# A hybrid decoder step on one core: the samples' recurrence moved to an earlier stage, gates by tanh, another order of loads and final stores

## What is computed

```python
u = _rmsnorm(tok, norm_mix[l]) @ w_in[l]
bg, cg, hv, q, fx, iv, og = jnp.split(u, SPLIT_POINTS, axis=-1)
y_conv = cg * conv            # conv: width 3 over bg * hv
f = lb + (1 - lb) * sigmoid(fx);  kk = 1 - f
S_new = exp(b_last) * S0 + k~^T v;  o = scores @ v + (q * exp(b)) @ S0
y_rec = rmsnorm_per_head(o) * rec_gain * silu(og)
h = h + concat(y_conv, y_rec) @ w_out
for e in range(32): out += combine[:, e] * (act(x @ w1[e] + b1[e]) @ w2[e] + b2[e])
y_prompt, y_sample = rmsnorm(h), also the new convolution rows and the new states
```

## Time and profile before

| | us |
|---|---|
| runs of the kernel before | 1114.75, 1112.18, 1114.08 |
| their median | 1114.08 |
| the profiled execution's own time | 1113.06 |
| its span, first to last instruction | 1111.3 |
| busy PE, weight loads, DVE, ACT, POOL | 1051.9, 465.3, 268.1, 171.5, 24.7 |
| bytes moved by DMA | 431.94 MB |
| granted clock of TensorE, mean | 0.994 of full |

### The profile page before, as it was taken

One profiled execution on the slowest core, in us unless ns is written; L12 is line 12 of the kernel. 1 busy time (PEld: TensorE's weight loads), 2 busy tenths in 40 slices (PEclk: granted clock), 3 DMA queues, 4 the chain that ended last, 5 costly groups with the idle time before them and its releaser, 6 DMA issues.

```text
span 1111.3 us, 12051 instructions
## 1 busy us (share of the span) xinstructions
PE 1051.9 (95%) x5212; PEld 465.3 (42%) x5212; DVE 268.1 (24%) x527; ACT 171.5 (15%) x412; POOL 24.7 (2%) x63
## 2 busy tenths in 40 slices
PE   7999999999999999999999989899998999999996
PEld 6767855343434334343433324243434343433332
DVE  5657634221111212020201012121212020202122
ACT  3562004120201011110110102020101010101102
POOL 3000012000000000000000000000000000000000
PEclk9999999999999999999999999999999999999998
DMA  9942379999999999999999999999999999999994
GB/s 304 354 177 76 143 277 392 408 428 427 428 428 426 429 426 428 428 427 428 428 427 428 425 431 426 427 428 427 429 428 427 429 426 428 425 431 426 429 420 170
DMA packets 50873, 431.94 MB, mean 389 GB/s; under 512 B 5238, under 2 KB 16190, under 8 KB 25120
## 3 DMA queue, kind: packets, MB, share of 16 engines
q1 hardware_dynamic: 48800, 428.54, 92.6%
q0 software_dynamic: 608, 2.04, 0.6%
q10 hardware_dynamic: 1408, 0.54, 0.2%
HBM read 427.63 MB, written 3.48 MB: 388 GB/s over the span
## 4 chain that ended last, share of the span: by engine, by line
PE 60%; DMA 36%; DVE 2%; issue 1%; ACT 0%; SPq 0%; DVEq 0%
DMA ring<-in_expert_w 35%; PE ps L1884 28%; PE ps L1939 8%; PE ps L1501 6%; PE ps L1806 3%; PE ps L1479 3%; PE ps L1780 2%; PE ps L1627 2%; PE ps L1569 1%; PE ps L1790 1%; PE ps L1859 1%; DMA ring<-in_x_prompt 1%; PE ps L1721 1%; PE ps L1808 0%; PE ps L1713 0%
## 5 line engine op out<-in xcount | busy, mean ns | idle before, releaser
L1884 PE MATMUL ps<-ring,mem 128*64 128x512 f32 x2048 | 461.7, 600 | 19.7 <-DMA ring<-in_expert_w 19.7
L1884 PEld LDWEIGHTS ps<-ring,mem 128*64 128x64 f32 x2048 | 146.1, 137 | 303.2 <-issue 302.1
L1939 PE MATMUL ps<-ring,mem 128*64 128x512 f32 x1024 | 223.7, 594 | 4.0 <-ACT mem L850 3.7
L1302 DVE TENSOR_TENSOR mem<-mem,ps 128x1024 f32<-128x1024 f32 x30 | 36.6, 1221 | 449.6 <-PE ps L1806 415.4
L1939 PEld LDWEIGHTS ps<-ring,mem 128*64 128x64 f32 x1024 | 72.3, 137 | 143.6 <-issue 136.1
L1501 PE MATMUL ps<-ring 128*128 128x266 f32 (+1 forms) x320 | 77.0, 397 | 2.0 <-DVE ring L970 1.5
L855 ACT ACTIVATE mem<-ps 128x264 f32<-128x264 f32 x16 | 6.3, 391 | 448.5 <-PE ps L1859 448.5
L1780 PEld LDWEIGHTS ps<-mem 128*128 128x128 f32 x600 | 65.4, 173 | 13.4 <-issue 12.2
L1780 PE MATMUL ps<-mem 128*128 128x128 f32 x600 | 70.1, 276 | 0.0
L1501 PEld LDWEIGHTS ps<-ring 128*128 128x128 f32 x320 | 60.6, 193 | 16.4 <-issue 3.9
L1806 PE MATMUL ps<-mem 128*128 128x512 f32 x120 | 60.0, 620 | 0.0
(11 more groups left out here) (295 smaller groups left out, 546.2 us busy)
## 6 DMA issues: line engine op xcount, KB each, us to landing
ring<-in_expert_w SPq DMA_DIRECT2D x182, 2048.0 KB, 39.8
ring<-in_expert_w SPq DMA_DIRECT2D x18, 1024.0 KB, 27.4
ring<-in_w_in SPq DMA_DIRECT2D x6, 2048.0 KB, 22.0
ring<-in_w_out SPq DMA_DIRECT2D x2, 2048.0 KB, 11.2
ring<-in_w_in SPq DMA_DIRECT2D x2, 1024.0 KB, 8.4
ring<-in_state_rec SPq DMA_DIRECT2D x4, 512.0 KB, 10.5
out<-ring SPq DMA_DIRECT2D x4, 512.0 KB, 13.3
ring<-in_expert_w SPq DMA_DIRECT2D x4, 512.0 KB, 22.6
```

The source lines that it names most:

```text
L1302: dve.tensor_tensor(h3[:, m], h3[:, m], ps[:, 4 + 2 * m:6 + 2 * m, :].rearrange("p a n -> p (a n)"), ALU.add)\
L1884: done = mm(ps[CAP * e:CAP * e + CAP, b, :], xgT3[:, t, CAP * e:CAP * e + CAP], ring[:, slot[e], col:col + HALF], start=False, stop=(t == ...
L1939: done = mm(ps[CAP * e:CAP * e + CAP, 4 + half, :], actT3[:, 4 * v + t, CAP * e:CAP * e + CAP], ring[:, slot[e], col:col + HALF], start=(v ...
```

## The change

- **Samples earlier.** `("s0", 0)` to `("s0", 3)` come at levels 1, 2, 4 and 5 instead of 4 to 7; `outer` 0 to 2 between the output gate's rows instead of between BG and HV; `os` before level 7 instead of behind CG 1, into banks 0 and 1; its sum is an entry of its own, `("osum", 0)`, behind BG 1.
- **Gates by tanh.** ACT makes tanh(x/2), DVE (t + 1) x in one instruction instead of three; the missing half goes into `grec` (one instruction of 128 x 4 at the start).
- **Loads.** The states are loaded before OG, BG and HV. The new states are stored right behind `load(0)`, and place 4 is the second place of `PLACES`, so that its load follows these stores. Six loads instead of five can be issued before PE is through with the scores and CG.
- **Small waits.** `nconv` moves before CG 3, `recur` 1 before CG 2; `mix` of the first tile waits for each part of the convolution alone; `state` waits for `os_sb`.
- **The end.** The root and the store of the samples come first (SP), and ACT stores all four quarters of `y_prompt`, behind its own scaling.

```diff
-PLACES = [0, 1, 2, 3, 8, 4, 9, 5, 6, 7, 10]
+PLACES = [0, 4, 1, 2, 3, 8, 9, 5, 6, 7, 10]
...
-        SCHEDULE += [("rows", (IV, 1, 0)), ("khat", 0)] + level(1) + [("rows", (IV, 1, 1))] + level(2)
+        SCHEDULE += [("rows", (IV, 1, 0)), ("khat", 0), ("s0", 0)] + level(1) + [("rows", (IV, 1, 1)), ("s0", 1)] + level(2)
...
+                if what == "osum":
                     dve.wait_ge(os_ps, HEADS)
...
             sp.wait_ge(og_ps, 3)
             load(0)
-            sp.wait_ge(hv_ps, 4)
-            load(1)
-            load(2)
...
             sp.wait_ge(snew_sb, 2 * HEADS)
             for h in range(HEADS):
                 sp.dma_start(new_rec_sample[0, :, h].rearrange("b k v -> k b v"), s0[:, h]).then_inc(state_out, 16)
+            sp.wait_ge(os_ps, HEADS)
+            sp.wait_ge(state_out, 16 * HEADS)
+            load(1)
...
-                    act.activation(sog3[:, i] if i < 2 else sogS, ps[:, 5 + i, 0:WIDE[i]], ACT.Exp, scale=-1.0)\
-                        .then_inc(og_exp, 1)
+                    act.activation(sog3[:, i] if i < 2 else sogS, ps[:, 5 + i, 0:WIDE[i]], ACT.Tanh, scale=0.5)\
+                        .then_inc(og_tanh, 1)
...
-                    link(dve.tensor_scalar(g, g, 1.0, None, ALU.add))
-                    link(dve.reciprocal(g, g))
-                    dve.tensor_tensor(g, g, ps[:, 5 + a, 0:WIDE[a]], ALU.mult).then_inc(sog_sb, 1)
+                    dve.scalar_tensor_tensor(g, g, 1.0, ps[:, 5 + a, 0:WIDE[a]], ALU.add, ALU.mult).then_inc(sog_sb, 1)
...
                     act.dma_start(y_prompt[0, P:2 * P, 0:HALF], fin3[:, 1, 0:HALF]).then_inc(out_done, 16)
+                    for nth, (i, at) in enumerate(((0, slice(0, HALF)), (1, slice(HALF, D)), (0, slice(HALF, D)))):
+                        act.wait_ge(fin_sb, nth + 2)
+                        act.dma_start(y_prompt[0, i * P:(i + 1) * P, at], fin3[:, i, at]).then_inc(out_done, 16)
```

More of the change, by code:

```diff
@@ L324, in build_step @@
         SCHEDULE = [("rows", (IV, 0, 0))] + DIAG[0] + [("rows", (IV, 0, 1))] + level(0)
-        SCHEDULE += [("rows", (IV, 1, 0)), ("khat", 0)] + level(1) + [("rows", (IV, 1, 1))] + level(2)
[L326 to L331, removed]
+        SCHEDULE += [("rows", (IV, 1, 0)), ("khat", 0), ("s0", 0)] + level(1) + [("rows", (IV, 1, 1)), ("s0", 1)] + level(2)
+        SCHEDULE += [("b1", 0), ("rows", (IV, 2, 0)), ("vdiag", 0)] + level(3) + [("rows", (OG, 0, 0)), ("s0", 2)]
+        SCHEDULE += level(4) + [("outer", 0), ("rows", (OG, 0, 1)), ("s0", 3)] + level(5) + [("outer", 1), ("rows", (OG, 1, 0))]
+        SCHEDULE += level(6) + [("gate", 0), ("outer", 2), ("rows", (OG, 1, 1))] + DIAG[1] + [("rows", (OG, 2, 0)), ("os", 0)] + level(7)
+        SCHEDULE += [("gate", 1), ("gate", 2), ("proj", (BG, 0)), ("proj", (HV, 0))] + level(8)
+        SCHEDULE += [("proj", (BG, 1)), ("osum", 0), ("proj", (HV, 1))] + level(9)
+        SCHEDULE += [("proj", (BG, 2)), ("qhat", 0), ("proj", (HV, 2))] + level(10) + [("state", 0)]
         SCHEDULE += [("proj", (BG, 3))] + level(11) + [("recur", 0), ("proj", (HV, 3))] + level(12)
-        SCHEDULE += [("proj", (CG, 0))] + level(13) + [("proj", (CG, 1)), ("os", 0), ("proj", (CG, 2))]
-        SCHEDULE += [("recur", 1), ("proj", (CG, 3))]
+        SCHEDULE += [("proj", (CG, 0))] + level(13) + [("proj", (CG, 1)), ("recur", 1), ("proj", (CG, 2)), ("nconv", 0)]
+        SCHEDULE += [("proj", (CG, 3))]
         def w_group(g):
@@ L477, in _ @@
                 sp.dma_start(new_rec_sample[0, :, h].rearrange("b k v -> k b v"), s0[:, h]).then_inc(state_out, 16)
+            sp.wait_ge(os_ps, HEADS)
+            sp.wait_ge(state_out, 16 * HEADS)
+            load(1)
+            sp.wait_ge(hv_ps, 4)
+            load(2)
+            load(3)
+            sp.wait_ge(cg_ps, 4)
+            load(4)
+            sp.wait_ge(score_sb, len(SCORES))
+            sp.wait_ge(nconv_step, 1)
+            load(5)
             sp.wait_ge(state_sb, 3)
@@ L773, in _ @@
                     exps(SCORES[a][1] + 2)
+                if what == "recur" and a == 0:
+                    act.wait_ge(os_sb, 1)
+                    act.activation(ssum[:, 0:P], oS, ACT.Square, accum_out=ossq[:, 8:9]).then_inc(osq_sb, 1)
                 if what == "recur":
@@ L894, in finish @@
                     square(n)
+                act.wait_ge(fsum_ps, c + 1)
+                act.activation(frstd[:, 2:3], ps[:, 7, 0:1], ACT.Sqrt, bias=eps_col, scale=1.0 / D).then_inc(frt_sb, 1)
                 root(3, 0)
@@ L1613, in _ @@
                         last.then_inc(os_ps, 1)
-            pe.wait_ge(bg_sb, 4)
-            pe.wait_ge(bx_sb, 4)
-            pe.wait_ge(nconv_step, 1)
-            for g in range(4):
-                last = pe.transpose(ps[0:2 + 2 * NS, 5, g * P:(g + 1) * P], nconv3[:, g], ident)
-            last.then_inc(nconv_step, 1)
+                if what == "nconv":
+                    pe.wait_ge(bg_sb, 4)
+                    pe.wait_ge(bx_sb, 4)
+                    pe.wait_ge(nconv_step, 1)
+                    for g in range(4):
+                        last = pe.transpose(ps[0:2 + 2 * NS, 5, g * P:(g + 1) * P], nconv3[:, g], ident)
+                    last.then_inc(nconv_step, 1)
             def mix(i, first, halves=(0, 1), steps=range(4)):
@@ L1626, in mix @@
                         k = t if first else 4 + t
+                        if first and i == 0 and n == 0:
+                            pe.wait_ge(yconv_sb, t + 1)
                         last = mm(ps[:, (6, 4)[i] + n, :], yT3[:, k, TILE_COL[i]:TILE_COL[i] + P],
```

72 lines of the change are left out of this document (27 added, 45 removed).

## The result

| | us |
|---|---|
| kernel before, 17 runs | median 1113.41 (1111.46 to 1115.57) |
| changed kernel, 17 runs | median 1116.24 (1113.71 to 1118.66) |
| ratio, with 95% interval | 1.0027 [1.002, 1.0035] |
| forecast, on the earlier median of 1114.08 | +1.3 (1115.4, range 1112.0 to 1118.2) |
| measured difference | +2.8 |

The change makes the kernel slower by 0.27%.

A forecast was written before the change was run, and what follows sets the result against it. The prediction took an unbroken stream of expert weights, started by PE's first release, to bound the kernel. Hole +2.1, gate -0.5 and end -0.3 gave +1.3 us: 1114.08 to 1115.4 us, range 1112.0 to 1118.2.

The forecast's parts named there:

- What bounds the kernel: Expert weights: one unbroken stream of transfers, starting with PE's first release; PE's delay before the pairs moves the end equally.
- Rival 3: Expert loads: the stream is bound by its bytes, so earlier loads gain some 8 us, to 1106; chance 0.08.
- The hole: PE ahead of level 4: the second head's scaling delays ACT's bias copy, so PE idles 2.1 us more.
- Rival 2: Mixer, level 4: no hole, for instance because ACT overlaps the scalings; 1111.7 to 1113.3 us, chance 0.17.
- the upper bound of 4.5: Mixer: the hole's cost in us if later levels lose the same again.
- the gate: Output gates: the shorter DVE work removes PE's wait ahead of HV 0, a gain of 0.48 us.
- the small waits: Wait ahead of mix moves to CG 3: gain 0, at most 0.24 us.
- The end: Final stores: samples first, bulk stores behind ACT's scaling; gain 0.3 us, between a gain of 1.9 and a loss of 1.5.
- Rival 1: Final stores: bulk stores behind ACT's scaling set a slower end, +1.5 us, besides the hole; 1117.2 us, chance 0.2.
- The sum: Whole kernel: +2.1 for the hole, -0.5 gate, -0.3 end, giving +1.3 us.
- within 0.2%: Measured outcome: no change distinguishable, less than 2.2 us either way; chance 0.62.

The follow-up runs named there:

- e12: e9 with the expert loads and the stores of new states put back to the kernel before's times; 1109.56 us, ratio 0.9968.
- e1: Changed kernel with only the second head's scaling moved back, behind vdiag instead of ahead of level 2; 1112.31 us, ratio 0.9993.
- e10: Changed kernel, hole included, with 8 and 6 products without use on PE ahead of its first projection; 1113.13 us, ratio 0.9997.
- e9: e7 with products without use on PE at the start, eight ahead of the first x tile and six ahead of the first projection; 1109.51 us, ratio 0.9965.
- e4: Kernel before with only the gates changed, tanh instead of exp; 1113.35 us, ratio 1.0.
- e7: e1 with the three bulk stores of y_prompt on SP behind the samples, only ACT's own quarter on ACT; 1112.91 us, ratio 0.9995.
- e8: Kernel before with only the states loaded early and the four state scalings at the changed kernel's places; 1115.64 us, ratio 1.0029.
- e6: Changed kernel with half of the second head's scaling ahead of the bias copy, the other half behind vdiag; 1112.91 us, ratio 0.9994.
- e2: Changed kernel with two products without use on PE in the hole ahead of level 4; 1115.81 us, ratio 1.0022.
- e5: e1 with the expert loads and the stores of new states put back to the kernel before's times; 1111.49 us, ratio 0.998.

## Why the prediction was right, and where not

**What bounds the kernel: right, with two rows misread.** L - R is 891.3 to 891.7 in all ten profiles that mark it, at R from 197.7 to 204.9, whatever else was changed. The time is PE's first release plus a constant, and every term ahead of it goes one to one into the end. Rival 3 (a stream bound by bytes that come early) is refuted by e12, and by after itself. The prediction took 10.3 us for the last of the first eleven loads; that was the one issued at 186.5. The one issued at 189.7 took 12.0 and landed at 201.7, so it came 2.8 us behind the first release and not 1.1, and the case against rival 3 was weaker than it looked. It is L - R that settles it: in after the last load landed 1.4 us behind the release (206.3), and the stream took 891.3 us all the same. The steady rate, too, begins with the ninth slice and not the eighth.

**The hole: right in place, chain and size.** Forecast 2.1, idle time 2.12, effect on R 2.3. Rival 2 (no hole) is refuted, and there was no second hole, which the upper bound of 4.5 allowed for.

**The step that failed is the price of that hole.** The sum charged the idle time alone. The prediction's steps took every product at the duration that its row of before has, which holds only while the granted clock stays at 1.00; a hole that the change makes can take that away from the products behind it. In the profiled execution it was 3.3 us, as much again as the hole and half more. That is most of what put the first half load at 204.85 instead of the forecast 200.5: 1.5 us came from the start of PE, and R - F rose by 4.5 where the terms of the forecast give 2.1 - 0.5 = 1.6. Over many executions it is less: after lies 3.9 above e1 and e10 3.6 above e9, so beyond the hole's 2.3 some 1.3 to 1.6 us, an estimate from medians whose intervals are about 1 us each.

**Small gains ahead of the pairs: mis-sized, low.** Predicted 0.48 for the gate and 0 for the small waits. Without the hole the change moves R - F from 168.58 to 167.47, by 1.11: 0.56 by the gate (e4), about 0.24 by the wait ahead of `mix`, whose row now has no idle time (the prediction's upper bound for it); 0.3 were not traced to a row.

**The end: right in sign, small in size.** Predicted 0.3, measured 0.7 between before and after and 1.1 as a mean of ten profiles. By the Trainium skill (Trainium Kernel Development and Optimization, Key Constraints), issuing from several queues saves issue time alone. The 1.2 that the prediction worked out beside it lies near, but e7 shows that issue time saved need not shorten the end. In after the bulk stores began where they were forecast, but ACT needed until 1113.86 for them, 2.9 us where 1.45 was forecast; the end came 2.4 us behind the last issue, as it had behind the small stores. In e7 the last issue came 1.3 us earlier behind L than in e1, and the end did not move. Rival 1, a slower end, is refuted by S - L. In the medians this gain isn't visible, and the runs leave that open.

**The sum.** With measured terms: +2.3 (hole) - 1.1 (R - F) - 0 to 1.1 (end) + 1.3 to 1.6 (clock) = +1.4 to +2.8, beside +2.8 measured. The measured 1116.24 lies within the forecast range, and the direction was right. That the number came within 1.5 us is in part luck: the missing term of the clock (+1.3 to +1.6) was partly offset by gains that were counted too low. The forecast made "within 0.2%" the likeliest, and the result is just past that line, 0.27%, for lack of the clock's term.

**What can be had.** The change without its hole is 0.8 us below before (e1, its interval reaches 1.0004). With products at the start it is 1109.51, 6.7 us below the changed kernel and 0.35% below the one before (0.9965 [0.9952, 0.9978]), the best of all that was run, together with e12.

## What to carry to other kernels

Moving work on an engine that looks idle is charged by the link that follows it in the same engine's list: here eight small ACT instructions ahead of one copy that DVE already waited for. If that opens a hole in TensorE's stream, price the hole and, beside it, what a fall of the clock may add to the products behind it, here from nothing to one and a half times the hole; a place a few entries later cost nothing here. For terms below the spread of the runs, compare the distance between two marks within one execution, which repeated here to hundredths of a microsecond.

## What the runs showed of the hardware

- The granted clock fell behind holes of 2.12 us in the changed kernel (3.3 us lost, twice; 1.7 in e10), not behind the same hole in e8, not behind 0.95 us in e6, nor when the hole was filled to 0.4. It also fell in routing with no new hole (e2 and e5, some 1.6 us). What decides between after and e8 isn't settled. In e8 the samples' outer products don't follow, but e10 has the same products as after, four microseconds earlier, and lost another amount.
- At the start the clock also fell without a hole of 2 us: in e6 and e8 it went to 0.50 at 12 to 13 us, in or just behind 1.49 us without a product, and was back near 15. With six products kept in that gap (e9 to e12) it stayed at 1.00.
- The first projection's 64 products took 16.7 to 18.3 us, and 15.33 in each of the four kernels that kept TensorE busy while the input came. In the windows of the changed kernel the clock column reads 1.00 at the start, while five products were counted in 14 to 18 us per window where ten or eleven is usual; in e6 it reads 0.50 there. A column of 1.00 in the first microseconds is thus not proof of the full rate; the durations are. The Trainium skill ("TensorE: Matmul & The Clock Gate", Part 1) warns that such records can be unreliable, and says that the engine starts at the low rate until activity releases it. Both agree with these rows: 1.00 in the column over products at half rate, and products that were slow at first in every profile.
